# Masked attention jobs in pairs on both row halves of the array, one key rotation, and a weight panel issued without a wait

## The chip, the cores and the metric

One core of a Trainium2 chip runs the whole program. The metric is the device time of one execution in microseconds, as the median of the runs. Everything is float32.

## The reference

Two transformer blocks follow each other on one sequence of T = 512 tokens with D = 1024 features. The parts that the change touches:

```python
# block 1: sliding window with sinks: 8 heads of 64, 2 key heads, window of 128
q = rope(rms_norm(q), pos); k = rope(rms_norm(k), pos)
s = einsum('bnqhgd,bnkhd->bnhgqk', qb, kband) * 64 ** -0.5    # 128 queries, 256 keys
s = where(allowed, s, -1e30)
p = softmax(concat([s, sink]))[..., :-1]
y_b = einsum('bnhgqk,bnkhd->bqhgd', p, vband) * silu(z_b)
# block 2: sparse attention: an index (4 heads of 64) picks 128 keys for each query
score = einsum('bqh,bqhs->bqs', wi, relu(einsum('bqhd,bsd->bqhs', qi, ki)))
sel = top_k(where(causal, score, -inf), 128)
p = softmax(where(valid, q @ k[sel] * 64 ** -0.5, -inf)); a_out = p @ v[sel]
# ki and k, one head of 64 each, are rotated by partial_rope (the first 16 features)
```

Block 1 also has a cross attention over 256 memory rows (4 heads of 128), and an RWKV-7 scan, whose decay, normalised keys and bonus, sum(r k r_k) v over each head, are made beside the attention. Block 2 has a causal convolution of 31 taps beside the sparse attention, a layer norm over it, then cross attention and a feed-forward part.

## The kernel before

Each engine runs a program of its own, written out by hand; there is no planner, and semaphores with counts tie them together. The order of instructions in one program is the order of its source. `h`, `q2`, `kd` and the like lie as features (partitions) by tokens. A head has 64 features, so two heads share the 128 partitions: `u_` = 0 or 1 is the half of the rows, `pair` the column.

*Attention.* TensorE, ScalarE and VectorE each have a helper `attention` that walks one list of jobs. A job of the window (`window_jobs`) is a block `b` of 128 queries and one pair of heads, so both halves of the rows: 4 blocks x 4 pairs = 16 jobs, after 8 jobs of the memory attention, which use all 128 rows. The sparse attention (`sparse_jobs`) has 24 jobs, 4 and 4 pairs in blocks 0 and 1 (128 and 256 keys) and 8 and 8 single heads in blocks 2 and 3 (384 and 512 keys). In step `i` TensorE issues the scores of job `i` (L723), a fill of dense work, the transposes of the probabilities of job `i - 2` (L735), a fill, the weighted values of job `i - 3` (L747), a fill, and what `inject` holds for the step. A fill is a number of `pairs` of matmuls of a dense product (L553, in the sparse stage L651) from a generator: (1, 1, 1) in the window stage, `sparse_fills` in the other. When a job changes from one half of the rows to the other, `other_rows` makes TensorE wait for its own last matmul.

*PSUM.* Banks 2 and 3 (`v`) take scores, 4 and 5 (`a`) transposes and sums, 6 and 7 (`o`) weighted values. `take_bank` takes them in turn and waits until the last but one taken of the kind has been read. VectorE's masked maximum (L1791) copies the scores out of the bank and so frees it; in memory jobs ScalarE's exponentials do, and VectorE passes the signal on. ScalarE makes the exponentials (L1295, L1296) and copies the transposes (L1306); VectorE normalises them (L1630) and takes the outputs (L1624, L1636).

*Work beside the window attention.* VectorE's `read_through` mixes tokens with their predecessors (`shifted`, L1624 and L1633, one tile in a step). `DECAY_AT` = (13, 16, 19, 22) are the steps after which TensorE issues `decay_sums(i)` (two single products, L705), and two steps later `bonus_sum(i)`, a product into a bank of kind `v`. At step 13 the sums of the key norms (L694) go ahead. On VectorE the key norms are applied after that (L1630, L1633), then for each of the four tiles a decay part (L1627, a scan L1897, products) and an applying part, whose last operation reads the bonus bank.

*Keys of block 2.* `kraw` holds the index key in one half of the rows and the attention key in the other. `single("v", con(name), kraw)` multiplies it with a constant 128 x 128 matrix: `dup1` and `dup0` copy one half to both, `rot2dup1` and `rot2dup0` do so rotated, `rot2` rotates in place. VectorE's `rope_dup` reads two such banks, multiplies by `trig`, and adds: `kid` in the index stage, `kd` in round 11 of the 16 rounds of top-k (L2203, L2204).

*Weights.* SyncE's program fills a ring of 4 panels of 512 KB (L2490). It waits for the memory input, which ScalarE's queue brings (L1317), ahead of panel 1; the four loads of x (L2485) go ahead of panel 2. The first dense product of all is `memory_keys` (L763), on panels 0 and 1 and on 2 and 3, once VectorE has the memory's squares.

## Time and profile before

| | us |
|---|---|
| median of 3 runs | 1723.69 (1723.01 to 1725.76) |
| profiled execution | 1725.95 |
| its span | 1724.1 |
| mean granted TensorE clock | 0.991 |

The span has four places that matter here: the start until 30, the memory and window attention from about 160 to 379, the index stage and top-k from about 888 to 991, and the sparse attention until 1108. Times below are microseconds from the span's start, lengths of instructions in the timelines too. A number ahead of an engine's name is the start, the next the length of the run of like instructions; matmuls overlap, so the next start says more than the length. The bracket at a row's end is the idle time ahead of it and what ended it.

### The profile page before, as it was taken

The numbers are of one execution on the slowest core, as the hardware profiler recorded it, in microseconds if no ns is written. First come the engines' busy times: TensorE is split into PE (matmuls) and PEld (weight loads), VectorE is DVE, ScalarE is ACT, GpSimd is POOL, SyncE is SP. The second block draws the span as 40 slices with busy tenths as digits, with TensorE's granted clock in tenths as the row PEclk, the third lists the DMA queues.
The fourth block names the chain that finished last, engine by engine and source line by source line (L and its number), as shares of the span: only waits on it lengthen the run. The fifth ranks groups of instructions, "written<-read, shape, count | busy, mean of one in ns | idle before, by whom it ended". The sixth has DMA issues, their size and how long they took to land.

```text
span 1724.1 us, 23185 instructions
## 1 busy us (share of the span) xinstructions
PE 1660.1 (96%) x9016; PEld 1084.0 (63%) x9016; DVE 1013.6 (59%) x2023; ACT 393.1 (23%) x767; POOL 132.2 (8%) x121
## 2 busy tenths in 40 slices
PE   6999998999999999899999999999999999999997
PEld 6445543445555555445854466747885888888885
DVE  3434946863323333245748989656667878787454
ACT  2344345431111111121115433220211000000000
POOL 0020200030000000000006800000000000000000
PEclk9999999999999999999999999999999999999999
DMA  6221111111110101111212121122112222223221
GB/s 249 74 73 61 62 49 37 49 49 38 38 50 26 50 28 48 68 64 71 85 74 72 63 74 66 57 74 73 49 49 89 83 89 83 98 74 98 86 91 68
DMA packets 45693, 119.93 MB, mean 70 GB/s; under 512 B 5073, under 2 KB 19153, under 8 KB 45201
## 3 DMA queue, kind: packets, MB, share of 16 engines
q1 hardware_dynamic: 44496, 113.79, 18.8%
q10 hardware_dynamic: 864, 3.35, 0.5%
q8 instruction: 72, 1.18, 0.3%
q0 software_dynamic: 224, 1.31, 0.2%
q14 instruction: 37, 0.29, 0.1%
HBM read 116.34 MB, written 2.10 MB: 69 GB/s over the span
## 4 chain that ended last, share of the span: by engine, by line
PE 86%; DVE 10%; ACT 2%; issue 1%; DMA 1%; SPq 0%; ACTq 0%; DVEq 0%
PE bank L553 30%; PE vpair L1107 4%; PE opair L1107 4%; PE bank L651 3%; PE bank L1107 3%; PE abank L1107 3%; PE vpair L723 3%; PE opair L583 2%; PE vpair L583 2%; PE abank L867 2%; PE vpair L867 2%; DVE arena L1633 2%; PE opair L1136 2%; PE opair L747 2%; PE vpair L1136 2%; PE bank L570 2%
## 5 line engine op out<-in xcount | busy, mean ns | idle before, releaser
L553 PE MATMUL bank<-h,ring 128*128 128x512 f32 x1120 | 516.2, 603 | 3.2 <-ACTq L1244 3.2
L553 PEld LDWEIGHTS bank<-h,ring 128*128 128x128 f32 x1120 | 204.8, 191 | 227.8 <-issue 218.2
L1624 DVE TENSOR_TENSOR arena<-arena,vpair 128x256 f32<-128x256 f32 x87 | 36.6, 421 | 190.3 <-PE vpair L867 118.3
L553 PE MATMUL bank<-arena,ring 128*128 128x512 f32 (+1 forms) x320 | 122.8, 519 | 0.0
L1624 DVE TENSOR_TENSOR arena<-ring 128x512 f32<-128x512 f32 (+2 forms) x112 | 63.7, 568 | 65.3 <-DMA ring<-weights 45.0
L1633 DVE SCALAR_TENSOR_TENSOR arena<-arena,cols 128x512 f32<-128x512 f32 (+1 forms) x133 | 97.9, 736 | 4.7
L553 PEld LDWEIGHTS bank<-arena,ring 128*128 128x128 f32 x320 | 57.2, 189 | 46.9 <-issue 43.4
L723 PE MATMUL vpair<-arena 128*128 128x256 f32 (+4 forms) x224 | 69.2, 414 | 4.4 <-DVEq L1620 2.4
L1624 DVE TENSOR_TENSOR arena<-arena 128x256 f32<-128x256 f32 (+1 forms) x114 | 58.3, 511 | 18.1 <-PE bank L763 10.5
L723 PEld LDWEIGHTS vpair<-arena 64*128 64x128 f32 (+1 forms) x224 | 37.2, 187 | 35.9 <-issue 19.8
L2474 POOL TENSOR_TENSOR arena<-arena 128x512 f32<-128x512 f32 x43 | 56.1, 1305 | 16.6 <-ACT arena L1497 13.4
L747 PE MATMUL opair<-arena 128*64 128x128 f32 (+1 forms) x368 | 52.8, 310 | 0.5 <-DVE arena L1636 0.3
L651 PEld LDWEIGHTS bank<-ring,arena 128*128 128x128 f32 x384 | 45.5, 191 | 11.3 <-issue 10.4
L747 PEld LDWEIGHTS opair<-arena 128*64 128x64 f32 (+1 forms) x368 | 37.8, 150 | 23.1 <-issue 14.9
L867 PEld LDWEIGHTS vpair<-arena 64*64 64x64 f32 x1152 | 36.7, 135 | 24.3 <-issue 24.3
L2453 POOL TENSOR_TENSOR arena<-arena,cst 128x256 f32<-128x256 f32 x40 | 31.1, 778 | 264.1 <-DVE arena L1624 261.5
L651 PE MATMUL bank<-ring,arena 128*128 128x128 f32 x384 | 50.6, 282 | 0.6 <-ACT arena L1248 0.6
L1296 ACT ACTIVATE arena<-arena,small 128x256 f32<-128x256 f32 (+3 forms) x64 | 33.4, 522 | 72.7 <-DVE small L1630 71.4
L867 PE MATMUL abank<-arena 64*64 64x64 f32 (+1 forms) x896 | 41.4, 231 | 7.3 <-DVE arena L1624 4.2
L867 PEld LDWEIGHTS abank<-arena 64*64 64x64 f32 x896 | 33.7, 134 | 21.9 <-issue 12.3
L1624 DVE TENSOR_TENSOR tmp<-sq 128x512 f32<-128x512 f32 (+1 forms) x12 | 7.2, 603 | 65.1 <-ACT sq L1221 64.9
L2442 POOL TENSOR_SCALAR arena<-arena 128x512 f32<-128x512 f32 x12 | 18.9, 1577 | 345.2 <-ACT arena L1239 345.2
(323 smaller groups left out, 2728.0 us busy)
## 6 DMA issues: line engine op xcount, KB each, us to landing
ring<-weights SPq DMA_DIRECT2D x185, 512.0 KB, 3.5
ring<-weights SPq DMA_DIRECT2D x68, 128.0 KB, 2.3
ring<-weights SPq DMA_DIRECT2D x40, 64.0 KB, 2.0
x<-xt SPq DMA_DIRECT2D x4, 512.0 KB, 6.8
out<-h SPq DMA_DIRECT2D x8, 256.0 KB, 2.0
cst<-cst_in ACTq DMA_DIRECT2D x1, 1504.0 KB, 11.5
arena<-memt ACTq DMA_DIRECT2D x1, 1024.0 KB, 6.3
arena<-mem2t POOLq DMA_DIRECT2D x1, 1024.0 KB, 5.1
```

What stands on the lines that cost most here:

```text
L553: last = mm(o[:, 0:n], weight(), src, start=c == 0, stop=c == len(srcs) - 1)
L570: last = mm(o[:, :], w[c], h[:, c, :], start=n == 0, stop=n == KD - 1)
L583: last = mm(o, lhs(k), rhs(k), start=k == 0, stop=k == 3)
L651: last = mm(o[:, t * n:(t + 1) * n], src[:, c, tok(t)], w[c][:, 0:n], start=c == 0, stop=c == KD - 1)
L723: last = mm(o[:, u_ * nk:(u_ + 1) * nk], a, b, start=c == 0, stop=c == len(parts) - 1)
L747: last = mm(view(o), vs, ps(pt), start=s == 0, stop=s == len(parts) - 1)
L867: last = mm(o[rows, j * n:(j + 1) * n], lhs[rows, j, :], rhs[rows, j, :], start=True, stop=True)
L1107: last = mm(o, lhs(c), rhs(c), start=c == 0, stop=c == 3)
L1136: last = mm(o, lhs(c), rhs(k), start=opens and k == 0, stop=closes and k == HF - 1)
L1624: do(V.tensor_tensor(out, a, b, op), sig)
L1633: do(V.scalar_tensor_tensor(out=out, in0=a, scalar=s, in1=b, op0=o0, op1=o1), sig)
L2474: do(G.tensor_tensor(acc, acc, cprod[:, k % 4], ADD), tap_added)
```

## The change

- A masked job is one half of the rows: two heads of the same half (window stage, and blocks 0 and 1 of the sparse one), or one head as before. There are as many jobs as before, and none changes halves. Its two heads' outputs lie side by side in 64 rows, so that weighted values are matmuls of 256 columns and VectorE takes 64 x 256 instead of 128 x 128.
- From job `first` on (8 in the window stage, 0 in the sparse one) two neighbouring jobs `i` and `i + 1`, one on each half, go together. Their scores are issued in turn, at even steps, after both banks have been taken; their weighted values too, four steps later and ahead of the transposes; VectorE takes both outputs in odd steps. At step 8 VectorE signals the bank of the last memory job early, after its `shifted`.
- `DECAY_AT` becomes (13, 17, 19, 22). The bonus sums fall on steps 15, 19, 21 and 24 (15, 18, 21 and 24 before).
- The keys of block 2 are multiplied by `rot2` once, and `rope_keys` makes `kid` and `kd` in the index stage by two products and four additions over 64 rows each. Nothing of the keys is left in round 11. Three of the four single products are gone.
- SyncE doesn't wait for the memory input.

Calls of `attention` that pass `first` on all three engines, and the lists that `inject` becomes, are left out of the diff, as are most removed lines that the listing above shows:

```diff
@@ -434,18 +434,20 @@
...
+                k0 = max(b - 1, 0) * P
+                nk = (b + 1) * P - k0
+                for kv in range(2):
+                    for u_ in range(2):
+                        rows, pairs = slice(64 * u_, 64 * u_ + 64), slice(2 * kv, 2 * kv + 2)
+                        score = [[(memq[rows, 2 * kv + i, tok(b)], skd[rows, kv, k0:k0 + nk])] for i in range(2)]
+                        pv = [(lambda o, rows=rows: o[rows, 0:2 * P],
+                               [(sv[:, k0 // P + s, kv * HD:kv * HD + HD], lambda pt, s=s: pt[:, 2 * s * P:2 * (s + 1) * P])
+                                for s in range(nk // P)])]
+                        mask = con("causal", 1) if b == 0 else con("band", 0, 2 * P)
+                        head = COLS["sinks"][0] + 4 * kv + u_
+                        jobs.append((nk, HD ** -0.5, score, mask, cols[:, head:head + 3:2], pv,
+                                     lambda o, rows=rows: o[rows, 0:2 * P].rearrange("p (i t) -> p i t", i=2),
+                                     yb[rows, pairs, tok(b)], yb[rows, pairs, tok(b)]))
@@ -464,16 +466,16 @@
...
+                n = 2 if b < 2 else 1
+                for p0 in range(0, 4, n):
+                    for u_ in range(2):
+                        rows, pairs = slice(64 * u_, 64 * u_ + 64), slice(p0, p0 + n)
+                        score = [[(q2[rows, p0 + i, tok(b)], kd[rows, 0:nk])] for i in range(n)]
+                        pv = [(lambda o, rows=rows, n=n: o[rows, 0:n * P],
+                               [(vwi[:, s, 0:HD], lambda pt, s=s, n=n: pt[:, n * s * P:n * (s + 1) * P]) for s in range(nk // P)])]
+                        jobs.append((nk, HD ** -0.5, score, mask, None, pv,
+                                     lambda o, rows=rows, n=n: o[rows, 0:n * P].rearrange("p (i t) -> p i t", i=n),
+                                     mix[rows, pairs, tok(b)], None))
@@ -489,9 +491,27 @@
...
+        def paired_with(j, first):
+            return j >= first and (j - first) % 2 == 0
+        def scored_in(i, n, first):
+            return [j for j in (i,) if j < min(n, first)] + [j for j in (i, i + 1) if paired_with(i, first) and j < n]
+        def weighed_in(i, n, first):
+            return [j for j in (i - 3,) if 0 <= j < first and j < n] + [
+                j for j in (i - 4, i - 3) if paired_with(i - 4, first) and j < n]
+        def taken_in(i, n, first):
+            return [j for j in (i - 4,) if 0 <= j < first and j < n] + [
+                j for j in (i - 5, i - 4) if paired_with(i - 5, first) and j < n]
...
-        DECAY_AT = (13, 16, 19, 22)
+        DECAY_AT = (13, 17, 19, 22)
@@ -706,23 +726,47 @@
...
+            def attention(jobs, work=iter(()), fills=even_fills, inject={}, first=99):
...
+                def scores(js):
+                    lists, lasts = [], []
+                    for j in js:
+                        nk, _, score, *_ = jobs[j]
...
+                        lists.append([(o[:, u_ * nk:(u_ + 1) * nk], a, b, c == 0, c == len(parts) - 1)
+                                      for u_, parts in enumerate(score) for c, (a, b) in enumerate(parts)])
+                    for both in zip(*lists):
+                        lasts = [mm(to, a, b, start=s, stop=e) for to, a, b, s, e in both]
+                    for last in lasts:
...
+                def weighed(js):
+                    lists, lasts = [], []
+                    for j in js:
+                        att["pt"] += 1
+                        pe.wait_ge(pt_ready.sem, att["pt"])
+                        o = take_bank("o")
+                        pt = bufs["att"][1][:, (att["pt"] - 1) % 2]
+                        lists.append([(view(o), vs, ps(pt), s == 0, s == len(parts) - 1)
+                                      for view, parts in jobs[j][5] for s, (vs, ps) in enumerate(parts)])
+                    for both in zip(*lists):
+                        lasts = [mm(to, a, b, start=s, stop=e) for to, a, b, s, e in both]
+                    for last in lasts:
+                        o_done.inc(last)
+                for i in range(n + 3):
+                    ready = weighed_in(i, n, first)
+                    scores(scored_in(i, n, first))
...
+                    if len(ready) == 2:
+                        weighed(ready)
@@ -736,19 +780,11 @@
...
+                    if len(ready) == 1:
+                        weighed(ready)
...
+                    for f in inject.get(i, ()):
+                        f()
@@ -810,10 +846,11 @@
...
-            inject = {}
+            inject = {i: [] for i in range(99)}
...
-                inject[DECAY_AT[i]] = lambda i=i: decay_sums(i)
-                inject[DECAY_AT[i] + 2] = lambda i=i: bonus_sum(i)
+                inject[DECAY_AT[i] + 2].append(lambda i=i: bonus_sum(i))
+                if i:
+                    inject[DECAY_AT[i]].append(lambda i=i: decay_sums(i))
@@ -1001,8 +1038,7 @@
...
-            single("v", con("dup1"), kraw)
-            single("v", con("rot2dup1"), kraw)
+            single("v", con("rot2"), kraw)
@@ -1016,9 +1052,6 @@
...
-            single("v", con("dup0"), kraw)
-            fill(work)
-            single("v", con("rot2dup0"), kraw)
@@ -1301,7 +1334,7 @@
...
-                            act.wait_ge(o_done.sem, st["pt"] - 2)
+                            act.wait_ge(o_done.sem, st["pt"] - 2 + (i >= 4 and paired_with(i - 4, first)))
@@ -1635,9 +1668,9 @@
...
-            def v_in():
+            def v_in(later=0):
...
-                dve.wait_ge(v_done.sem, st["v"])
+                dve.wait_ge(v_done.sem, st["v"] + later)
@@ -1761,24 +1794,29 @@
...
-            def rope_dup(dst):
-                o = v_in()
-                tt(tmp[:, 0], o[:, :], trig[:, 1], MUL, v_read)
+            def rope_keys():
+                tt(tmp[:, 0], kraw, trig[:, 1], MUL)
...
-                tt(dst, tmp[:, 0], tmp[:, 1], ADD, rope_done)
-            def attention(jobs, stage_=(), todo=(), fills=even_fills, after={}):
+                for dst, rows in ((kid, slice(64, 128)), (kd, slice(0, 64))):
+                    for u_ in range(2):
+                        tt(dst[64 * u_:64 * u_ + 64, :], tmp[rows, 0], tmp[rows, 1], ADD, rope_done if u_ else dve_chain)
+            def attention(jobs, stage_=(), todo=(), fills=even_fills, after={}, first=99):
...
+                    if i == first and i:
+                        dve.wait_ge(exp_done.sem, st["att"])
+                        signal_now(v_read)
...
-                        o = v_in()
+                        o = v_in(paired_with(i, first))
@@ -1801,7 +1839,7 @@
...
-                        if mask is None:
+                        if mask is None and i != first:
@@ -1810,10 +1848,10 @@
...
-                    if i >= 4:
-                        _, _, _, _, _, _, view, dst, gate = jobs[i - 4]
+                    for j in taken_in(i, n, first):
+                        _, _, _, _, _, _, view, dst, gate = jobs[j]
...
-                        dve.wait_ge(o_done.sem, st["o"])
+                        dve.wait_ge(o_done.sem, st["o"] + paired_with(j, first))
@@ -2177,7 +2215,8 @@
...
-            rope_dup(kid)
+            dve.wait_ge(dense_act.sem, reads("act", start["index"] + 2))
+            rope_keys()
@@ -2197,7 +2236,6 @@
...
-                    rope_dup(kd)
@@ -2478,8 +2516,6 @@
...
-                if p == 1:
-                    sp.wait_ge(mem_in.sem, 16)
```

## Rows read from the trace of the kernel before

**Rows 1.** The page, part 1: busy time, share of the span and instructions of each engine.

```profile
PE 1660.1 (96%) x9016; PEld 1084.0 (63%) x9016; DVE 1013.6 (59%) x2023; ACT 393.1 (23%) x767; POOL 132.2 (8%) x121
```

**Rows 2.** Timeline of TensorE, 0 to 45: start, length, engine, line, operation, tiles, count, [idle before].

```profile
7.93 8.55 PE L763 MATMUL bank<-arena,ring 128*128 128x256 f32 x32 [7.93 <-DVE arena L1630]
...
22.32 9.88 PE L763 MATMUL bank<-arena,ring 128*128 128x256 f32 x32 [5.40 <-DMA ring<-weights]
```

**Rows 3.** Queues' timelines, 0 to 30, and the DMA view: slices of 0.75 us, issues.

```profile
0.73 7.05 SPq L2490 DMA_DIRECT2D ring<-weights  x2
...
1.16 0.45 ACTq L1317 DMA_DIRECT2D arena<-memt  x1
...
GB/s 0 0 120 235 420 441 382 426 337 56 0 104 404 404 404 268 333 306 404 366 369 412 459 449 403 409 456 435 361 409 412 410 418 404 219 27 0 0 0 0
...
arena<-memt ACTq DMA_DIRECT2D x1, 1024.0 KB, 6.3
```

**Rows 4.** Busy time by window: length, each engine's busy time, granted clock, DMA share, GB/s.

```profile
21.00:27.80 6.80, 5.49 (x13) 4.41 (x14) 0.00 (x0) 2.16 (x4) 0.00 (x0) 0.50 0.73 293
```

**Rows 5.** Timeline of TensorE, 246 to 312: row-half and column-half matmuls.

```profile
249.33 1.45 PE L723 MATMUL vpair<-arena 64*128 64x256 f32 x4
250.71 1.99 PE L553 MATMUL bank<-h,ring 128*128 128x512 f32 x4
...
301.25 1.13 PE L705 MATMUL abank<-arena 64*128 64x512 f32 x4
...
307.55 0.67 PE L747 MATMUL opair<-arena 128*64 128x128 f32 x8
```

**Rows 6.** Timeline of TensorE, 264 to 384: where steps begin, and waits.

```profile
264.27 3.84 PE L694 MATMUL abank<-sq,cst 128*128 128x512 f32 x8
...
288.12 1.45 PE L723 MATMUL vpair<-arena 64*128 64x256 f32 x4 [0.57 <-DVE small L1791]
291.95 3.78 PE L553 MATMUL bank<-h,ring 128*128 128x512 f32 x4 [2.38 <-ACTq L1244]
...
344.47 1.45 PE L723 MATMUL vpair<-arena 64*128 64x256 f32 x4
...
378.89 0.69 PE L857 MATMUL vpair<-arena 64*64 64x64 f32 x32
```

**Rows 7.** Timeline of VectorE, 262 to 300: starts of the parts of its chain.

```profile
273.85 0.43 DVE L1630 TENSOR_SCALAR tmp<-sq 128x512 f32<-128x512 f32 x1
...
278.84 0.43 DVE L1627 TENSOR_SCALAR arena<-arena 128x512 f32<-128x512 f32 x1
...
284.14 0.75 DVE L1633 SCALAR_TENSOR_TENSOR arena<-arena,cols 128x512 f32<-128x512 f32 x1
...
285.65 0.69 DVE L1624 TENSOR_TENSOR tmp<-arena 128x512 f32<-128x512 f32 x1
...
290.00 0.69 DVE L1633 SCALAR_TENSOR_TENSOR arena<-arena 128x512 f32<-128x512 f32 x1
...
292.90 0.69 DVE L1624 TENSOR_TENSOR arena<-vpair,arena 128x512 f32<-128x512 f32 x1
```

**Rows 8.** Timeline of TensorE, 884 to 1000: dense work without a wait.

```profile
912.96 39.75 PE L553 MATMUL bank<-h,ring 128*128 128x512 f32 x92
```

**Rows 9.** Busy time by window: window stage, key rotation in the top-k rounds, sparse stage.

```profile
264.20:378.90 114.70, 109.80 (x375) 48.24 (x373) 83.91 (x203) 53.66 (x119) 8.91 (x6) 0.97 0.12 42
968.86:971.89 3.03, 3.03 (x8) 1.33 (x8) 2.92 (x3) 1.09 (x2) 2.87 (x3) 1.00 0.01 3
999.40:1087.40 88.00, 85.14 (x480) 58.28 (x480) 82.07 (x191) 28.99 (x75) 0.00 (x0) 1.00 0.20 72
```

**Rows 10.** Waits of VectorE, 985 to 1140 (us, times, longest), and TensorE's timeline there.

```profile
DVE arena L1791 <- PE vpair L723: 4.1, 4, 1.8
...
DVE arena L1636 <- PE opair L747: 2.8, 2, 2.2
...
1108.55 3.70 PE L1032 MATMUL bank<-arena,cst 128*128 128x512 f32 x8
```

More of the change, by code:

```diff
@@ L707, in _ @@
             att = {"p": 0, "pt": 0}
-            def attention(jobs, work=iter(()), fills=even_fills, inject={}):
+            def attention(jobs, work=iter(()), fills=even_fills, inject={}, first=99):
                 n = len(jobs)
@@ L823, in first_decay @@
                 decay_sums(0)
-            inject[7] = rotated
+            inject[7].append(rotated)
             assert KK_AT == DECAY_AT[0]
-            inject[KK_AT] = first_decay
+            inject[KK_AT].append(first_decay)
             pe.wait_ge(wa2_in.sem, 16)
-            attention(memory_jobs() + window_jobs(), work, inject=inject)
+            attention(memory_jobs() + window_jobs(), work, inject=inject, first=8)
             finish(work)
@@ L1050, in _ @@
             work = cross_kv()
-            attention(sparse_jobs(), work, sparse_fills, {26: conv_mean})
+            attention(sparse_jobs(), work, sparse_fills, {26: [conv_mean]}, first=0)
             pe.wait_ge(o_read.sem, state["o"])
@@ L1272, in read_through, with attention @@
                     reading["done"] += 1
-            def attention(jobs, stage_=(), todo=(), fills=even_fills, before={}):
+            def attention(jobs, stage_=(), todo=(), fills=even_fills, before={}, first=99):
                 n = len(jobs)
@@ L1410, in _ @@
                       [lambda n=n: silu_in(yb[:, n]) for n in range(4)] + [lambda n=n: raw_tile(n) for n in range(1, 13)] +
-                      [lambda n=n: silu_in(ya[:, n]) for n in range(4)], before=before)
+                      [lambda n=n: silu_in(ya[:, n]) for n in range(4)], before=before, first=8)
             act.wait_ge(head_done.sem, 4)
@@ L1551, in _ @@
                       [lambda n=n: copy_dense(v2[:, :, tok(n)], dense_in()[:, 0:M].rearrange("p (s d) -> p s d", s=2)) for n in range(8)],
-                      sparse_fills)
+                      sparse_fills, first=0)
             conv_squares()
@@ L1937, in _ @@
             attention(memory_jobs() + window_jobs(), FILL1, [None] * 4 + [lambda n=n: shifted(n) for n in range(1, 13)] + [None] * 4,
-                      after=after)
+                      after=after, first=8)
             reading = {"done": 0, "todo": gated_todo(GATES)}
@@ L2247, in _ @@
             after.update({i: (lambda i=i: conv_taps(4 if i < 16 else 3)) for i in range(SEL, 25)})
-            attention(sparse_jobs(), CROSSKV, [None] * 16, sparse_fills, after)
+            attention(sparse_jobs(), CROSSKV, [None] * 16, sparse_fills, after, first=0)
             assert st["tap"] >= len(rest)
```

44 lines of the change are left out of this document (1 added, 43 removed).

## The prediction

> **What bounds the kernel now.** First the page: TensorE is busy 96% of the span [rows 1], so a part of the change that takes time off TensorE could pay, unless the stage in which it lies has another end. So I went to the four places that the diff touches and asked in each who waits last.
>
> The start, in TensorE's timeline: the first key product of the memory begins at 7.93, as soon as VectorE has the squares; a second one, from panel 2 of the ring, begins at 22.32 after 5.40 idle for a DMA [rows 2]. The DMA rows say why: panel 1 isn't issued until the memory input has landed (issued 1.16, 6.3 to land), x and panel 2 stand behind it in the same program, and the slices of 0.75 us show a hole, 56, 0 and 104 GB/s, between two plateaus of about 400 [rows 3]. After the idle time the granted clock of 21.0 to 27.8 is 0.50, 1.2 GHz [rows 4].
>
> The window stage, 264.2 to 378.9: TensorE 109.80 of 114.70 us busy, VectorE 83.91 [rows 9]. TensorE sets the pace by step, but VectorE's chain of decay work sets it by rounds; TensorE waited 0.57 and then 2.38 behind it, and the four matmuls after that took 3.78, where four like them take 1.99 [rows 5, 6]: the clock fell to its lower level.
>
> The sparse stage, 999.4 to 1087.4: VectorE 82.07 busy in 191 instructions, TensorE 85.14 of 88.00 [rows 9]. The 5.9 us that VectorE isn't busy are 191 gaps of 0.03, so VectorE is without a break, though its busy share is the lower. TensorE's work there is dense products as filling, which have no reader in a hurry. VectorE is the bound; it waits only 4.1 us for scores at the stage's head and 2.8 us for weighted values at its tail [rows 10].
>
> **The change part by part.** The sum is made against the profiled execution: 1725.95 us, its span 1724.1; it lies 2.26 over the median of the runs, 1723.69, and 0.19 over the highest of them (1723.01 to 1725.76).
>
> *Start (panel 1 no longer waits).* Panels 1, x, 2 and 3 are issued from 1.2 on, beside the memory input. By 4.9, with two queues at work, panel 0 (0.52 MB) and what the other queue had moved (columns 0.17 MB and some 0.33 of the memory, from the plateau's rate) are nearly equal, so I take equal shares. The memory's last 0.7 MB then go at half of about 420 GB/s, until 8.3 to 8.8, 1.1 to 1.4 later than 7.4 [rows 3]. TensorE starts at 9.2 rather than 7.93, its 8.4 us of keys and the sum's product end at 18.2. Panel 2 is by then 1.05 (two panels) + 2.1 (x) + 0.52 MB plus the other queue's part down the line, about 14.7: there, since 18.2 is later. So the second keys start at 18.2, not 22.3, and at full clock: 92 matmuls of 512 columns in 39.75 [rows 8] make 0.216 for 256 columns, so the 32 take 6.9, to 25.1, where before they took 9.88, to 32.2 [rows 2]. **-7.1**; ends -2 (x and four panels share with constants that the chain needs at 25) and -8.
>
> What the rows show is that two queues together moved what one alone did and split it about evenly [rows 3]. The Trainium skill says the same in "DMA: Bandwidth & Descriptors", section "Queues, rings and completion order": each DMA engine goes round the queues that have work. It speaks against this part: the freed panels take half of the memory's rate. By it the loss is the 1.1 to 1.4 us already in the sum; the trace agrees.
>
> *Cost of one pair of jobs.* Before, the scores of one job are four matmuls of 64 rows by 256 columns, 1.38 to the next start, two on one row half and then two on the other, with about 0.1 before and 0.1 after them as the array changes halves: 1.57 a job, 3.14 a pair [rows 5]. After, the two jobs alternate halves. That two halves overlap is seen in the line that issues four matmuls of 64 by 512 in turn: 1.13 in all, where one after another at 0.216 per 256 columns they would take 1.73 [rows 5]. So a pair is about 1.24: **1.9 saved**. With 128 keys 2.30 becomes 0.76, with 384 and 512 keys (single heads) 2.0 and 2.45 are saved. Weighted values: eight of 128 columns take 0.67 now [rows 5], already less than 8 x 0.107; after, a pair has eight of 256 columns on two column halves, 1.22 against 1.58: 0.36 saved.
>
> That row is also where a rule speaks against the change: the Trainium skill, "TensorE: Matmul & The Clock Gate", "The mechanism", has weight loads overlap running matmuls only when the row group differs, and the two jobs' weighted values differ in columns alone. By it a pair of weighted values would cost some 0.9 more; where VectorE sets the end that is hidden, but the pair ahead of the sums of step 13, the three behind the window stage's last wait and the last of the sparse stage would show it: +4.5, 1713.7. The row of eight in 0.67 [rows 5] disagrees, and I go by the row.
>
> In all TensorE sheds 2 x (1.54 + 0.33) + 6 x (1.9 + 0.36), about 17 us, in the window stage, and by the same prices 26 in the sparse one. What comes of that:
>
> *Window stage.* I walk it step by step. At step 8 the first pair needs both score banks, and VectorE signals the second only after its `shifted`: 1.57 lost. Steps 8 to 13 then save 1.54 + 1.54 + 1.90 in scores and 0.8 in weighted values, which leaves the sums of step 13 4.2 earlier than 264.27 [rows 6]: 260.1. VectorE's parts, read off as differences of starts [rows 7]: normalising 5.0 (273.85 to 278.84), decay 6.8 (to 285.65), `shifted` with one job's softmax 4.35 (to 290.00), of which `shifted`, two operations on 512 columns like the one of 0.69, is 1.5, applying 3.7 (290.00 to the end of the bonus bank's read at 293.6). With two outputs taken in odd steps and none in even ones, a softmax is 2.51 and 3.43. Sums of step 13 end at 265.1, scores of 14 and 15 at 266.3; VectorE: 268.9, 273.9, 280.7 (product for the bonus at 279.9), 282.2, 285.6, and its read of the bonus bank ends at 289.2. The bonus sum takes one of the two score banks. Before, the next job took the other and ran on (288.12 [rows 6]); after, the next *pair* (16 and 17) needs both, and waits until 289.2. TensorE has ended steps 14, 15 and the bonus by 280.8: **8.4 idle**, and the clock is then half for a while, +2.75 as before [rows 6]. From there the round is VectorE's: decay sums after step 17 end at 306.5; decay 6.8, two `shifted` 3.0, softmaxes 5.9, applying 3.7 are 19.2 to 19.4, so pair 20 waits until 325.7 (3.6 idle) and pair 22 until 345.1 (4.8 idle). Job 22 began at 344.47 before [rows 6]. From pair 22 on there are 34.4 us to the stage's end at 378.89 [rows 6], less 1.9 for the scores of 22 and 23, the weighted values about even (three pairs where five single jobs were): 377.6 at full clock, 380.4 at half behind the third wait. Between -1.3 and +1.5 I take **+0.3**; ends -1.3 and +5 (half clock behind all three waits). So the 17 us that TensorE saves come back as 16.8 of waiting.
>
> *Key rotation.* Three products of 512 columns, two instructions and 0.86 each [rows 8], go from TensorE; VectorE has three operations fewer within its top-k rounds, where a window over just these shows 3.03 [rows 9]. VectorE runs on without a break from the top-k to the attention: **-3.0** there, -0.86 in the index stage, where VectorE waits for TensorE's products. The three more additions that the index stage gets are 64 rows each, under 0.7, and lie in VectorE's waits there.
>
> *Sparse stage.* VectorE starts 3.9 earlier. Of its 4.1 us of waits for scores [rows 10], paired scores leave about 1.7 (-2.4 with the three small ones at the end: 0.11, 0.38), its larger takes of outputs cost 8 x 0.135 = +1.1, and of the waits at the end and the drain behind the last probabilities about 4.8 go, as the last two jobs' products come together: the average of the convolution, now at 1108.55 [rows 10], starts near 1098.5. **-10.0** with the rotation's part; ends -6 and -12. Behind it the chain (squares, variance, output product) is untouched.
>
> Sum: 1725.95 - 7.1 + 0.3 - 10.0 = 1709.2.
>
> **The rivals.** *B, the clock falls more often.* Paired steps bunch the dense work; idle gaps of 2 to 3 us in each pair would come with VectorE as pace-maker, and the clock fell after idle times of 5.40 and 2.38 [rows 2, 6]. Speaks for it: VectorE rules both stages. Against: filling covers all but the named waits. It gives back some 7: 1716. *C, TensorE's saving counts in full*, as 96% busy [rows 1] would have it: 1725.95 - 7.1 - 17 - 26 - 3 = 1673; against it stand VectorE's gapless rows. *D, the start gains nothing*, because the memory stands behind seven transfers: 1716. *E, slower.* The waits at 16, 20 and 22 leave the clock at its lower level through steps 16 to 26, some 47 us of matmuls at full clock: up to +24, 1733. It decides once the stage has lost the 17 us of the other parts, 34 us spent at half clock; against it, the clock came back within 7 us each time (21.0 to 27.8 [rows 4]). *F, the change doesn't do what it says*: halves don't overlap in the scores. Against the row of four in 1.13 [rows 5] it would cost 1.57 a pair: three pairs ahead of the sums of step 13, which VectorE's rounds pass on, +4.7; the pair behind the last wait with its joint start, +3; the head of the sparse stage, +2: 1719.
>
> The Trainium skill, "TensorE: Matmul & The Clock Gate", "HAM oscillation — how this bites in real kernels", has a clock that falls anew at each wait between bursts of work. That is B and E, 1716 and 1733; rows 2 to 6 show single falls after waits and no train of them, hence B's 0.2 and E's 0.03.
>
> **How the numbers follow.** Main forecast 0.57, B 0.2, D 0.1, F 0.05, C 0.05, E 0.03. The low end takes all terms at theirs, 1725.95 - 8 - 1.3 - 12 = 1704.7, and 2 for the end of the median run under the profiled one: 1703. The high end has the start at -2 and the sparse stage at -6, or the window at +5 and the sparse stage at -6 (1714 to 1718), which takes in B and D. This kernel's measurement can tell 0.2%, 3.4 us, from no change: faster (under 1720.2) 0.93; same 0.04, the upper part of B, D and F; slower 0.03, E.
>
> **What the profile after would show.** TensorE's second keys start near 18 with no 5 us idle and no half clock; three waits on a VectorE read of the score bank ahead of the pairs 16, 20 and 22, of 8.4, 3.6 and 4.8 us; rows of the scores near 1.2 per eight matmuls of 256; window stage ending as late as before, less the start's gain; the convolution's average 17 earlier in all; from there everything shifted alike. I would be wrong if TensorE runs through the bonus sums, if the memory lands after 10, or if half clock shows outside the first wait.

## The result, and the profile after

The changed kernel takes 1711.75 us (median of 5 runs, 1709.19 to 1716.37) against 1723.69: a ratio of 0.9935, 95% interval 0.9914 to 0.9955. The forecast was 1709.2 in 1703 to 1718. It was added up from the profiled execution of the kernel before, 1725.95, which lies 2.26 over the median of its runs; from median to median it forecast 14.5 us less, and 11.9 came.

Two profiled executions of the changed kernel are at hand. Execution A is the one taken with the result (1716.27 us, span 1714.5), execution B comes from a later set of runs (label `e11_changed_again`, 1709.08 us, span 1707.3). These two letters have nothing to do with the rivals B to F of the prediction. The executions differ by 7 us, and where they differ is part of the answer. Stage lengths, each from the start of one operation to that of the next in TensorE's timeline (the top-k ends with VectorE's last round; step 8 is counted from where TensorE is free for it, which in A and B is 1.67 ahead of its first matmul):

| stretch | before | A | B | forecast of the change |
|---|---|---|---|---|
| start to step 8 of the window attention | 219.63 | 214.08 | 214.15 | -7.1 |
| step 8 to the window attention's end | 159.26 | 161.91 | 158.96 | +0.3 |
| to the index stage's single products | 508.97 | 508.87 | 506.25 | 0 |
| index stage's products | 10.45 | 9.59 | 9.58 | -0.86 |
| index scores to the last round of top-k | 92.31 | 89.32 | 89.33 | -3.0 |
| to the convolution's average | 117.93 | 113.45 | 113.46 | -6.1 |
| to the output product's last groups | 29.73 | 29.72 | 29.73 | 0 |
| to the end | 585.85 | 587.54 | 585.83 | 0 |
| span | 1724.1 | 1714.5 | 1707.3 | -16.8 |

The page of A, busy times and the granted clock in 40 slices, beside [rows 1]:

```profile
PE 1623.9 (95%) x8930; PEld 1068.2 (62%) x8930; DVE 1014.6 (59%) x2023; ACT 393.3 (23%) x767; POOL 132.5 (8%) x121
...
PEclk9999998999999999999999999999999999999999
```

TensorE has 36 us less to do (1660.1 before), and the time falls by 10: most of the saving is idle time now.

**The start.** TensorE's timeline of A, then the DMA view (slices of 0.75 us; issue to landing), beside [rows 2, 3]:

```profile
9.57 9.65 PE L799 MATMUL bank<-arena,ring 128*128 128x256 f32 x32 [9.57 <-DVE arena L1663]
19.06 0.59 PE L725 MATMUL abank<-arena,cst 128*128 128x256 f32 x2
19.49 7.07 PE L799 MATMUL bank<-arena,ring 128*128 128x256 f32 x32
26.40 7.31 PE L671 MATMUL bank<-ring,arena 128*128 128x128 f32 x64
```

```profile
GB/s 0 0 66 262 402 410 431 350 431 437 404 387 378 437 421 410 415 415 415 404 404 446 386 385 465 433 322 379 292 322 360 246 76 60 11 0 55 246 360 432
...
arena<-memt ACTq DMA_DIRECT2D x1, 1024.0 KB, 7.9
```

The hole of 56, 0 and 104 GB/s is gone; the memory input lands 7.9 after its issue, not 6.3; the second keys follow the first without a break. The first keys, though, take 9.49 from start to the sum's product, where they took 8.39. The windows say why (columns as in [rows 4]; [rows 2] has the start of the keys before), A and then before:

```profile
9.57:14.40 4.83, 4.83 (x11) 3.88 (x12) 4.44 (x12) 2.92 (x7) 0.00 (x0) 1.00 1.03 417
14.60:19.40 4.80, 4.80 (x24) 4.23 (x23) 0.82 (x2) 0.00 (x0) 0.00 (x0) 1.00 1.05 418
```

```profile
7.93:10.60 2.67, 2.67 (x6) 2.19 (x7) 2.46 (x7) 2.48 (x6) 0.00 (x0) 1.00 0.76 272
```

In A 11 matmuls take 4.83, 0.44 each, and from 14.6 on 24 take 4.80, 0.20 each: the program begins at half speed. (The clock column shows 1.00 in both rows, though the same matmuls take twice as long in the first; the durations decide. VectorE isn't what slows them: it delivers eight inputs in 3.08, 0.385 each.) Before, 2.67 us of matmuls ran so; in A it is nearly 5, by which the start loses 1.1. How long this lasts varies between executions. In the three traces of kernels that wait, whose keys begin at 7.9 to 8.0, the first keys take 8.39 to 8.85; in the eleven that don't, beginning at 9.5 to 10.0, they take 8.67 to 10.05, 9.39 in the middle. So some 0.6 of the loss goes with the later start as far as these traces tell, and the rest of A's 1.1 may be chance.

**The window stage.** TensorE's timeline of A, beside [rows 5, 6]:

```profile
215.75 0.71 PE L745 MATMUL vpair<-arena 64*128 64x128 f32 x8 [1.67 <-DVEq L1653]
...
284.62 2.08 PE L745 MATMUL vpair<-arena 64*128 64x256 f32 x8 [8.26 <-DVE arena L1657]
286.63 3.78 PE L573 MATMUL bank<-h,ring 128*128 128x512 f32 x4
...
302.28 1.03 PE L745 MATMUL vpair<-arena 64*128 64x256 f32 x8
...
305.16 1.08 PE L760 MATMUL opair<-arena 128*64 128x256 f32 x8
...
321.49 1.79 PE L745 MATMUL vpair<-arena 64*128 64x256 f32 x8 [2.03 <-DVE arena L1657]
...
341.42 1.26 PE L745 MATMUL vpair<-arena 64*128 64x256 f32 x8 [3.76 <-DVE arena L1657]
...
375.99 0.69 PE L894 MATMUL vpair<-arena 64*64 64x64 f32 x32
```

The three waits of the forecast are there, each on VectorE (the line is that of its helper; that it is the read of the bonus bank is shown by the experiments below): 8.26, 2.03 and 3.76 us where 8.4, 3.6 and 4.8 were said (0.58 more stands ahead of a decay sum at 318), and 1.67 at step 8. Eight score matmuls of a pair take 0.96 to the next start (302.28 to 303.24, where the next dense matmuls begin), eight of weighted values 1.01 (305.16 to 306.17): both halves do overlap, and by more than the 1.24 and 1.22 that I took. After the first wait the pair's scores take 2.08, at half clock:

```profile
284.60:291.10 6.50, 6.48 (x16) 2.97 (x18) 3.67 (x12) 1.79 (x6) 0.00 (x0) 0.50 0.00 0
214.08:375.99 161.91, 143.73 (x453) 65.77 (x453) 106.43 (x279) 73.48 (x170) 9.13 (x6) 0.94 0.14 46
```

```profile
214.15:373.11 158.96, 141.51 (x452) 65.14 (x452) 106.41 (x279) 73.49 (x170) 9.14 (x6) 0.95 0.14 47
```

The first row is the stretch behind the first wait, the second and third are the stage in A and in B. TensorE has 10 us (A) and 12 us (B) less to do than before (154.01 busy in 159.26), with the matmuls at half clock counted in, and the stage is as long as before or longer. The clock falls behind more than the first wait: a pair's scores, four dense matmuls and a pair's weighted values take 3.89 at full clock (302.28 to 306.17), and behind the three waits they take 7.09, 5.65 and 5.65 in A, 5.52, 6.65 and 3.99 in B. That is 6.7 us lost to the clock in A and 4.5 in B.

**Top-k and sparse attention.** VectorE alone from the index scores to the top-k's last round, in A and in the kernel before:

```profile
894.45:983.77 89.32, 87.69 (x222) 37.46 (x222) 77.76 (x176) 45.75 (x69) 60.47 (x49) 1.00 0.21 66
```

```profile
898.31:990.62 92.31, 90.66 (x226) 39.17 (x226) 79.65 (x174) 45.72 (x69) 61.98 (x50) 1.00 0.19 69
```

That is the 3.0 of the key rotation. All engines from VectorE's first softmax to the convolution's average, in A and before, and the longest wait of TensorE in A there:

```profile
983.80:1097.20 113.40, 92.92 (x653) 72.48 (x651) 104.72 (x248) 39.73 (x104) 3.01 (x3) 0.98 0.24 78
```

```profile
990.66:1108.55 117.89, 114.86 (x676) 82.22 (x674) 103.77 (x249) 39.69 (x104) 1.64 (x2) 1.00 0.20 71
```

```profile
PE vpair L745 <- DVE small L1829: 14.5, 9, 2.6
```

TensorE's busy time falls by 21.9 us, the stage by 4.5. VectorE has 104.72 busy and 248 gaps, which at the 0.031 of [rows 9] make 112.4 of 113.4; before it was 103.77 and 249 gaps, 111.5 of 117.9. Of 6.4 idle it keeps 1.0. TensorE waits 14.5 us in 9 places until VectorE has read the scores.

**Behind it.** The output product in A and in B:

```profile
1126.94 8.83 PE L1097 MATMUL vpair<-arena,ring 128*128 128x512 f32 x16 [1.99 <-DVE arena L1666]
```

```profile
1121.46 7.13 PE L1097 MATMUL vpair<-arena,ring 128*128 128x512 f32 x16 [1.99 <-DVE arena L1666]
```

The same 16 matmuls behind the same wait of 1.99 us take 8.83 in one execution and 7.13 in the other. In A the clock fell after that wait, in B it didn't. The kernel before took 7.13 there, as B did.

The 2.6 us between the window and the index stage are of the same kind. They lie in two places that the change doesn't touch, in A first and then in B:

```profile
625.37:631.95 6.58, 6.58 (x65) 4.00 (x65) 5.25 (x10) 0.00 (x0) 3.71 (x5) 0.74 0.00 1
711.92:718.35 6.43, 6.43 (x9) 2.62 (x10) 2.08 (x3) 0.00 (x0) 1.31 (x2) 0.55 0.56 204
```

```profile
622.48:627.51 5.03, 5.03 (x64) 2.89 (x65) 4.53 (x9) 0.00 (x0) 2.33 (x3) 1.00 0.01 2
707.48:712.84 5.36, 5.36 (x9) 2.08 (x10) 2.07 (x3) 0.00 (x0) 1.31 (x2) 0.68 0.61 212
```

The same matmuls take 6.58 at a mean clock of 0.74 and 5.03 at 1.00, and then 6.43 at 0.55 and 5.36 at 0.68. The profile before has both falls as A has them, so this difference belongs to the execution and not to the change.

### The profile page after: what moved, and what is told of

It reads as the page before. It is cut to its first block, busy times and chain, and to the rows that moved or that the text cites. A ratio compares the mean times of both kernels' runs of the same rounds, so it can differ in the third digit from the quotient of the medians.

```text
span 1714.5 us, 23030 instructions
## 1 busy us (share of the span) xinstructions
PE 1623.9 (95%) x8930; PEld 1068.2 (62%) x8930; DVE 1014.6 (59%) x2023; ACT 393.3 (23%) x767; POOL 132.5 (8%) x121
## 4 chain that ended last, share of the span: by engine, by line
PE 78%; DVE 18%; ACT 2%; issue 1%; DMA 0%; ACTq 0%; DVEq 0%
PE bank L573 26%; DVE arena L1666 5%; PE vpair L1140 4%; PE opair L1140 4%; PE abank L1140 3%; PE bank L1140 3%; DVE arena L1657 3%; PE opair L603 2%; PE vpair L603 2%; PE abank L904 2%; PE vpair L904 2%; PE opair L1169 2%; PE vpair L1169 2%; PE bank L590 2%; PE abank L603 2%; DVE arena L2242 2%
## 5 line engine op out<-in xcount | busy, mean ns | idle before, releaser
L745 PE MATMUL vpair<-arena 128*128 128x256 f32 (+4 forms) x224 | 45.8, 418 | 32.6 <-DVE small L1829 14.5
L745 PEld LDWEIGHTS vpair<-arena 64*128 64x128 f32 (+1 forms) x224 | 30.1, 195 | 48.5 <-DVE small L1829 16.8
L904 PEld LDWEIGHTS abank<-arena 64*64 64x64 f32 x896 | 33.7, 134 | 21.9 <-issue 12.2
L671 PE MATMUL bank<-ring,arena 128*128 128x128 f32 x384 | 46.7, 277 | 0.6 <-ACT arena L1281 0.6
L760 PE MATMUL opair<-arena 128*64 128x128 f32 (+2 forms) x288 | 43.7, 355 | 3.4 <-ACT arena L1339 2.0
L1463 ACT ACTIVATE arena<-abank 128x256 f32<-128x256 f32 x40 | 15.4, 384 | 125.1 <-PE abank L904 125.1
```

The source lines that it names most:

```text
L671: last = mm(o[:, t * n:(t + 1) * n], src[:, c, tok(t)], w[c][:, 0:n], start=c == 0, stop=c == KD - 1)
L745: lasts = [mm(to, a, b, start=s, stop=e) for to, a, b, s, e in both]
L760: lasts = [mm(to, a, b, start=s, stop=e) for to, a, b, s, e in both]
L904: last = mm(o[rows, j * n:(j + 1) * n], lhs[rows, j, :], rhs[rows, j, :], start=True, stop=True)
```

## The experiments

Ratios are to the kernel before on the same chip, with 95% intervals. The changed kernel stands at 0.9935 [0.9914, 0.9955] and 0.9932 [0.9918, 0.9945].

### The start

The wait put back into the changed kernel:

```diff
             for p in range(NPANEL):
+                if p == 1:
+                    sp.wait_ge(mem_in.sem, 16)
```

> The changed kernel with one edit undone: SyncE again waits for the memory input ahead of panel 1. If the start's gain is what the trace of the changed kernel shows (the end of the second key product 5.6 us earlier), the time is 5.6 above the changed kernel's 1711.75, about 1717.4; by the predicted 7.1 it would be 1718.9. If the start gains nothing that lasts (rival D), it is 1711.8. TensorE's second key product should begin near 22.3 again, behind 5 us of idle time, with the granted clock at 0.5 after it.

Measured: 1716.21, ratio 0.9956 [0.9941, 0.9972], 0.0021 to 0.0024 or some 4 us above the changed kernel, less than the 5.6 expected, with intervals that overlap a little: by itself the time decides little. TensorE's timeline has the idle time and the slow matmuls back:

```profile
7.86 8.93 PE L799 MATMUL bank<-arena,ring 128*128 128x256 f32 x32 [7.86 <-DVE arena L1663]
...
22.67 10.04 PE L799 MATMUL bank<-arena,ring 128*128 128x256 f32 x32 [5.45 <-DMA ring<-weights]
```

The other way round, the wait taken out of the kernel before:

```diff
             for p in range(NPANEL):
-                if p == 1:
-                    sp.wait_ge(mem_in.sem, 16)
```

> The kernel before with one edit: SyncE doesn't wait for the memory input. The end of TensorE's second key product came 5.6 us earlier in the changed kernel and 6.1 later again when the wait was put back. If all of it lasts, the time is 5 to 6 us under the kernel before of the same chip, a ratio of 0.997; the predicted 7.1 would give 0.9959; none, if some later transfer or the sums of x set the start, 1.000.

Measured: 1718.80 against 1724.03, 0.9969 [0.9957, 0.9981]: 5.3 us faster.

```profile
9.50 8.98 PE L763 MATMUL bank<-arena,ring 128*128 128x256 f32 x32 [9.50 <-DVE arena L1630]
...
18.74 7.07 PE L763 MATMUL bank<-arena,ring 128*128 128x256 f32 x32
25.65 7.31 PE L651 MATMUL bank<-ring,arena 128*128 128x128 f32 x64
```

The second keys end at 25.65, where those of [rows 2] ended at 32.03 (the next product's start): 6.4 earlier, and step 8 of the window attention begins at 213.26, 6.4 earlier too. The start's gain is real and it lasts, so rival D is out. The traces put it at 5.5 to 6.4 us; the time alone, 3.3 to 7.4 by its interval, wouldn't exclude 7.1.

### The window stage

Jobs still of one row half, but issued singly, with the old steps:

```diff
-        DECAY_AT = (13, 17, 19, 22)
+        DECAY_AT = (13, 16, 19, 22)
-            attention(memory_jobs() + window_jobs(), work, inject=inject, first=8)
+            attention(memory_jobs() + window_jobs(), work, inject=inject)
```

> The changed kernel with window jobs still made of one row half each, but every job issued alone, and with the decay steps of before (13, 16, 19, 22). If pairing gives its saving back in waits on the score bank that the bonus sum holds, the three waits (8.3, 2.0, 3.8 us) and the half clock behind them are gone, TensorE's extra matmul time comes back in their place, and the stage from step 8 to its end takes about 159 us as before, not 162: some 3 us under the changed kernel, 1709. If pairing pays in this stage (17 us less for TensorE), the time is well above 1715.

Measured: 1707.61, 0.9912 [0.9891, 0.9934], 4 us under the changed kernel, though the two intervals overlap. From step 8 to the stage's end:

```profile
214.29:371.59 157.30, 154.42 (x453) 70.25 (x453) 106.94 (x278) 74.34 (x172) 9.15 (x6) 0.99 0.14 47
```

157.30 with 154.42 busy: TensorE does 11 us more than in A and ends earlier. By this stage's length the pairing, with the decay step that moved for it, costs 1.7 us against B and 4.6 against A, and the regrouping by halves alone gains some 2 us on the 159.26 of before. (Half clock was expected to be gone and isn't: a wait of 2.10 is there, and the four dense matmuls behind it take 3.12.)

Then the bank. VectorE's applying part, its read of the bonus bank first:

```diff
+                o = v_in()
+                tt(bonus[:, i, :], o[:, :], v[:, i, :], MUL, v_read)
                 stt(kk[:, i, :], kk[:, i, :], -1.0, E[3], MUL, MUL)
...
                 tt(r[:, i, :], r[:, i, :], E[1], MUL)
-                o = v_in()
-                tt(bonus[:, i, :], o[:, :], v[:, i, :], MUL, v_read)
```

> The changed kernel, with VectorE reading the bonus bank as the first of the five operations of its applying part rather than the last, so the bank comes free 2.9 us earlier in each of the four rounds; nothing else moves. If the score bank held by the bonus sum sets the pace, the three waits fall from 8.3, 2.0 and 3.8 us to about 5.4, 0 and 0.9 and the time falls by 6 to 9 us, to 1703 to 1706. If VectorE's chain of decay work sets the pace whatever the bank does, the waits turn up elsewhere and the time stays at 1711 to 1712.

Measured: 1706.60, 0.9904 [0.9886, 0.9923]. TensorE's waits for the bonus bank, and the stage:

```profile
281.32 2.08 PE L745 MATMUL vpair<-arena 64*128 64x256 f32 x8 [5.34 <-DVE arena L1657]
...
334.42 1.74 PE L745 MATMUL vpair<-arena 64*128 64x256 f32 x8 [4.36 <-DVE arena L1657]
```

```profile
213.71:368.98 155.27, 141.46 (x453) 65.49 (x453) 106.06 (x279) 73.49 (x170) 8.66 (x6) 0.97 0.14 48
```

The first wait is shorter by 2.92, the second is gone, and the third is not shorter but longer, 4.36: the rounds come sooner, and the time won in the second is partly handed to the third. The stage takes 155.27, 3.7 under B and 6.6 under A. By the ratios the time falls by 5 us, a little less than the 6 to 9 expected.

With that, the third and fourth bonus sums behind the last pair's scores:

```diff
-        DECAY_AT = (13, 17, 19, 22)
+        DECAY_AT = (13, 17, 21, 23)
```

> The changed kernel with the bonus bank read first, as in the earlier run, and the decay steps at 13, 17, 21 and 23, so that the third and fourth bonus sums (steps 23 and 25) come after the last pair's scores and hold no bank that a pair waits for. If the bank is what costs, the third wait (4.36 us) and the half clock behind it go and the time falls by another 3 to 5 us under that run. If VectorE's chain sets the end, its last round now ends a step later and TensorE waits for it at the end of the stage: no gain, or up to 5 us lost.

Measured: 1703.97, 0.9876 [0.9861, 0.9890].

```profile
281.30 2.08 PE L745 MATMUL vpair<-arena 64*128 64x256 f32 x8 [5.35 <-DVE arena L1657]
...
314.88 1.13 PE L745 MATMUL vpair<-arena 64*128 64x256 f32 x8 [1.87 <-DVE arena L1657]
```

```profile
213.67:367.53 153.86, 142.27 (x452) 65.46 (x452) 107.53 (x279) 73.49 (x170) 8.57 (x6) 0.97 0.14 48
```

Two waits are left, 5.35 and 1.87, and the stage takes 153.86, 1.4 less. By the medians the time fell by 2.6, by the ratios by 4.8, for the 3 to 5 expected. The second wait isn't lost time: pair 20 begins at 314.9 in both runs, and the decay sums that filled TensorE's time ahead of it now come later. A part of what the third wait cost comes back as a fall of the clock near the end, where four dense matmuls take 3.33 (at 347.85) behind gaps of 0.53 and 0.28. It ran again beside the changed kernel:

> The kernel with late bonus sums again, beside the changed kernel: if what the two earlier runs showed holds, 7 to 10 us under the changed kernel.

> The changed kernel as it is, beside these kernels on the same chip, to have its own distance from each: 1712 to 1715, and a ratio near 0.9935 to the kernel before.

Measured on one chip: 1704.14 (0.9883 [0.9868, 0.9897]) and 1711.48 (0.9932): 7.3 us apart. This version beats both kernels, by 20 us the one before.

Last, the first bonus sum two steps later, in the kernel with late sums:

```diff
         DECAY_AT = (13, 17, 21, 23)
+        BONUS_AT = (17, 19, 23, 25)
...
-                inject[DECAY_AT[i] + 2].append(lambda i=i: bonus_sum(i))
+                inject[BONUS_AT[i]].append(lambda i=i: bonus_sum(i))
...
-                before[DECAY_AT[i] + 2] = lambda i=i: decay_exps(i)
+                before[BONUS_AT[i]] = lambda i=i: decay_exps(i)
...
-                after[DECAY_AT[i] + 2] = lambda i=i: decay_apply(i)
+                after[BONUS_AT[i]] = lambda i=i: decay_apply(i)
```

> The kernel with late bonus sums, and the first bonus sum moved from step 15 to 17, with the work that hangs on it on ScalarE and VectorE. If the first wait (5.35 us ahead of the pair 16) is long because VectorE has the key norms (5.0) and the decay part (6.8) to do before it can read, the pair 16 finds its banks free, the wait at 18 is 2 to 3 us, and the time falls by 2 to 4 us under that kernel's 1703.97. If the rounds behind it start later by as much, nothing is gained.

Measured: 1705.79, 0.9899 [0.9886, 0.9912], beside 1704.14 for the kernel with late sums on the same chip. Nothing gained, against my expectation:

```profile
278.35 2.08 PE L746 MATMUL vpair<-arena 64*128 64x256 f32 x8 [4.19 <-DVE small L1830]
282.02 3.78 PE L574 MATMUL bank<-h,ring 128*128 128x512 f32 x4 [1.60 <-ACTq L1278]
...
317.08 1.13 PE L746 MATMUL vpair<-arena 64*128 64x256 f32 x8 [3.50 <-DVE arena L1658]
```

```profile
213.90:368.79 154.89, 142.11 (x453) 65.31 (x452) 107.28 (x277) 73.50 (x170) 8.82 (x6) 0.96 0.15 48
```

The pair 16 waits still, 4.19 and then 1.60, though no bonus sum holds a bank now. The first wait's releaser is VectorE's masked maximum of the jobs ahead (L1830 in this kernel). So the first wait was never the bonus bank's alone: VectorE comes late out of step 14, where it has the key norms and a decay part (11.8 us, [rows 7]) ahead of the next scores. Pair 16 began at 284.62 in A, at 281.30 with the bank read first, and begins at 278.35 here, so about 6.3 us hung on the bonus bank, with the order of VectorE's work that it imposes, and moving the bonus sum away doesn't bring the pair earlier than that. What is won there is lost again behind it: 1.60, and 3.50 ahead of pair 20.

Whether the pairs pay in this stage once the bank is out of their way can be told by length only: 153.86 in pairs with late sums, 157.30 for single jobs. Single jobs with the bonus bank read first were not run.

### The sparse stage

Sparse jobs issued singly, on all three engines as here on TensorE:

```diff
-            attention(sparse_jobs(), work, sparse_fills, {26: [conv_mean]}, first=0)
+            attention(sparse_jobs(), work, sparse_fills, {26: [conv_mean]})
```

> The changed kernel with the sparse jobs, still of one row half each, issued alone. If VectorE sets the sparse stage's end, TensorE's 26 us come back as filled waits and only the head, the tail and the drain cost again: 3 to 6 us above the changed kernel, 1715 to 1718. If TensorE's time counted in full (rival C), it would be about 1738.

Measured: 1719.59, 0.9968 [0.9957, 0.9979], by the ratios 6 us above the changed kernel (7.8 by the medians, which come from different sets of runs). Rival C, full count of TensorE's time, is out. Then less work for VectorE, 22 of its taps left out in the kernel before and in the changed one:

```diff
-            rest = ... for i in range(2, 4) for w in range(TAPS)]
+            rest = ... for i in range(2, 4) for w in range(TAPS) if w not in range(15, 26)]
-            ... conv_taps(4 if i < 16 else 3) ...
+            ... conv_taps(3 if i < 16 else 2) ...
```

> The kernel before, with 22 of the 65 convolution taps that VectorE does beside the sparse attention left out (the convolution's result is then another one), and one tap less per step, so VectorE sheds 22 x 0.75 = 16.5 us there. If both engines are close to the bound before the change (TensorE busy 85.14 of 88.00), TensorE then sets the stage's end and little is gained: 3 to 5 us. If VectorE alone is the bound, 16.5 us.

> The changed kernel with the same 22 taps left out. If pairing took TensorE's 26 us out of the stage and only VectorE's work keeps them from showing, nearly all of the 16.5 us appear, 13 to 16 (about 1697), since TensorE idles 14.5 us in waits for VectorE's reads of scores. If TensorE's savings aren't there, 3 to 5 us as in the kernel before.

Measured: 1719.42 (0.9962 [0.9948, 0.9977]) and 1696.86 (0.9838 [0.9822, 0.9855]). By the ratios the first is 6.6 us under the kernel before, for 3 to 5 expected, and the second 16 to 17 under the changed kernel (14.9 by the medians); falls of the clock elsewhere in the program are in these numbers, so the stage decides. The stage from VectorE's first softmax to the convolution's average, for the unpaired jobs, for the kernel before with fewer taps, and for the changed one with fewer taps:

```profile
983.66:1102.64 118.98, 116.30 (x658) 83.57 (x656) 103.98 (x250) 39.73 (x104) 3.03 (x3) 1.00 0.21 74
```

```profile
988.22:1101.90 113.68, 113.27 (x676) 82.58 (x675) 87.22 (x228) 39.70 (x104) 1.67 (x2) 1.00 0.21 73
```

```profile
980.30:1078.96 98.66, 90.25 (x653) 71.67 (x652) 88.20 (x226) 39.73 (x104) 3.02 (x3) 1.00 0.26 90
```

Unpaired: 118.98, TensorE busy 116.30, so that regrouping alone gains nothing here (117.89 before). Fewer taps before: 113.68, TensorE 113.27, so that the same 16.5 us shed by VectorE gave 4.2, and TensorE is now the bound. Fewer taps after: 98.66 from 113.45, 14.8 of the 16.5, with VectorE filled but for 3.5 (88.20 and 226 gaps, 95.2). This is the clearest of the runs: before the change both engines were near the bound, and not VectorE alone, as the prediction had it; the change took TensorE 22 us away from it and left VectorE there.

### The key rotation

The rotation of before in the changed kernel:

```diff
-            single("v", con("rot2"), kraw)
+            single("v", con("dup1"), kraw)
+            single("v", con("rot2dup1"), kraw)
...
+            single("v", con("dup0"), kraw)
+            single("v", con("rot2dup0"), kraw)
...
-            rope_keys()
+            rope_dup(kid)
...
                     for i in range(4):
                         rope(q2[:, i, :], q2[:, i, :])
+                    rope_dup(kd)
```

> The changed kernel with the key rotation of before: four single products, one addition of 128 rows for each key, the second key's in round 11 of the top-k. By the prediction it costs 0.86 in the index stage and 3.0 in the top-k rounds, 3.9 in all, and the attention behind shifts with them as VectorE runs without a break: 1715 to 1716. If TensorE or the shared end hides it, under 1.

Measured: 1715.43, 0.9938 [0.9923, 0.9952]. In ratio it can't be told from the changed kernel's 0.9935 and 0.9932, nor from one that costs 3.9 us. In the trace it is there: the index stage's products take 10.45 again (9.59), and VectorE's stretch 92.32 (89.32):

```profile
893.01:985.33 92.32, 90.71 (x232) 39.36 (x232) 79.68 (x174) 45.74 (x69) 62.01 (x50) 1.00 0.20 69
```

The median is where it was expected, but on a chip whose kernel before stood at 1726.01, and each interval is some 2.6 us wide to either side. The 3.9 us are shown by the stages, not by the time.

## Why the prediction was right, and where not

- *Start, -7.1: mis-sized, -5.5.* The mechanism held: no hole, no wait, no half clock at 22. The second keys took 6.91 as worked out. What failed is the step "TensorE starts at 9.2, its 8.4 us of keys": it starts at 9.57, since the memory took 7.9 and not 7.1 to 7.6, and the keys take 9.49, since the clock begins at half and stayed so 2 us longer. I had taken the 8.39 of before over as a fixed length; the first six matmuls in it ran at half speed, and that part differs from one execution to the next. The last 0.2 is a slip of reading: the keys before made way for the next product at 32.03, not 32.2.
- *Pairs: 1.24 and 1.22 forecast, 0.96 and 1.01 measured.* The direction was right. The rule of the Trainium skill ("TensorE: Matmul & The Clock Gate", "The mechanism") that weight loads overlap running matmuls only when the row group differs, by which I had priced a pair of weighted values 0.9 higher, doesn't hold for this shape: eight matmuls of 256 columns on two column halves in 1.01 are 0.126 each, where 0.216 is one alone [rows 8].
- *Window stage, +0.3: right, and by its mechanism.* -0.3 in B, +2.65 in A. The three waits come where they were said, 14.6 us in all with the one of 0.58 for 16.8 (13.9 in B). The clock was mis-sized: 2.75 was taken for one fall, and 6.7 were lost in A, where all three waits brought one, and 4.5 in B, where the first two did. That waits too long and a fall too cheap nearly cancel in B is luck. TensorE's own saving was put at 17 us, and its busy time fell by 10 and 12, half clock counted in. What the forecast missed is how cheap the cure is: reading the bank first and moving two sums gave 7 us. And the first wait is only in part the bank's: pair 16 came 6.3 us earlier with the bank free, and waited 4.19 still.
- *Index and rotation, -0.86 and -3.0: right,* 0.86 and 2.99.
- *Sparse stage, -6.1 beside the rotation: mis-sized, -4.5.* VectorE is the bound, as the taps show; its larger takes cost 1.0 (104.72 for 103.77) as forecast. Before, it had 6.4 idle in the whole stretch, of which 5.4 went. The step that failed is the 2.4 of waits and 4.8 of drain, 7.2 in all, more than there was to take: the sum over VectorE's gaps would have bounded it. And VectorE was not the bound alone: before the change 16.5 us less for it brought only 4.2.
- *Rivals.* C and D are excluded by runs, F by the rows of pairs. Rival B, the clock: it does fall more often in the window stage, and not in a way that costs in the sparse one, where execution B ran with a mean of 0.95 and A with 0.98 and both took 113.4. In single executions it reaches its price all the same: two of the five runs of the result lie at 1716, A among them, and two near 1712. E didn't come: each fall ended after some us.
- *A sign of being wrong came.* "Half clock outside the first wait" was one of my signs. It shows behind the other waits of the window stage and, in A, in the output product. It spoke against the size of the clock's term, and the forecast of the time survived it. The convolution's average came 11.3 earlier in A and 18.9 in B, for 17.
- *The spread.* The changed kernel's runs lie 7 us apart, and so do A and B: 2.95 in the window stage, 2.6 between it and the index stage, 1.7 behind the output product's wait. In the window stage A loses 1.6 and 1.7 more behind the first and third waits and 1.0 less behind the second, and its third wait is 0.7 longer; in the other places the rows show a lower clock on the same matmuls. Why the clock falls in one execution and not in the other stays open. That B's span is the forecast's to 0.1 us is partly luck: a start and a sparse stage short by 3.2 together, against 2.7 of fewer falls than in the profile before, which nobody had forecast, and 0.6 in the window stage.

## What to carry to other kernels

Work taken off an engine that is 95% busy counts only where no other chain is as near to the bound; add up the other engine's busy time and its gaps over the stage, and what is left of the stage is the most that can come. When two jobs are issued together they need two buffers at once, so every single user of that ring of buffers becomes a barrier: read such a buffer first, or place its user behind the last pair. And a wait of 2 us on TensorE may cost twice, once for itself and once for the clock behind it, in some executions and not in others.

## What was not expected of the hardware

- TensorE's first matmuls of the program run at half speed: 11 in 4.83 us in A, 6 in 2.67 before. How many do varies between executions: the same first keys, begun at 9.5 to 10.0, took 8.67 to 10.05 us in eleven traces. Those of the three that began near 7.9 took 8.39 to 8.85, so a later start may cost some, but three are few.
- The same wait of 1.99 us was followed by a fall of the clock in A (8.83 for 16 matmuls) and by none in B (7.13). Runs of the changed kernel on one chip spread over 7.2 us (1709.08 to 1716.30), and those of the kernel before there over 5.3 (1720.78 to 1726.06): so a spread of several us was there before the change.
- Matmuls of 128 rows and 64 columns on the two column halves in turn take 0.126 us for 256 columns, near the 0.12 of those on row halves.
